# A layer's attention with its bookkeeping moved: another order of the modulation products, and the wide transposes copied out by two engines

## The reference

```
for i in range(DEPTH):                       # DEPTH = 2
    mods = sc @ ada_w[i] + ada_b[i]          # ada_w[i]: 1024 x 6144
    cmods = scc @ ada_w[i] + ada_b[i]
    x, xc = layer(x, xc, mods, cmods, ..., i < DEPTH - 1)

# in layer:
yb = conformer_conv(b_v, b_g, conv_b, conv_b_bias, cln_g, cln_b)
yc = window_attention(apply_rope(q_heads(c_q), cos, sin), apply_rope(kv_heads(c_k), cos, sin),
                      kv_heads(c_v), kc_c, vc_c, sink)
yd = global_attention(apply_rope(rms_norm(q_heads(d_q), qn_g), cos, sin),
                      apply_rope(rms_norm(kv_heads(d_k), kn_g), cos, sin),
                      kv_heads(d_v), kc_d, vc_d)
x_new = x + g1 * (jnp.concatenate([ya, yb, yc, yd], axis=-1) @ w_out)
```

## Time and profile before

| | us |
|---|---|
| median of three runs | 2913.59 |
| lowest and highest run | 2912.88, 2919.2 |
| the profiled execution | 2919.2 |
| its span in the trace | 2917.4 |
| attention of layer 0 (heads, flips, values) in the span | 221 to 397 |
| attention of layer 1 | 1315 to 1434 |

### The profile page before, as it was taken

The page is one execution under the profiler, slowest core; times in us unless marked ns, Lnnn a source line. Parts: engine busy times, 40 slices in busy tenths (PEclk is TensorE's granted clock), DMA queues, the critical chain, the costliest instruction groups (busy, mean ns, idle before and its releaser), DMA issues.

```text
span 2917.4 us, 35242 instructions
## 1 busy us (share of the span) xinstructions
PE 2636.4 (90%) x13904; PEld 1501.9 (51%) x13904; DVE 1283.0 (44%) x2508; ACT 979.0 (34%) x1825; POOL 334.1 (11%) x185
## 2 busy tenths in 40 slices
PE   5999897799999997796869999998699997999998
PEld 3875553323333322584534333332477686787886
DVE  2496514234444444476342232332656555343342
ACT  4216522233444443526422222221334333322222
POOL 0210001001111001120010000000013320121121
PEclk9999999799999999799989999999899998999999
DMA  6117723599999999320028999999221002232321
GB/s 244 58 58 261 256 77 130 198 322 350 348 360 361 345 347 317 106 73 1 15 94 331 386 387 386 387 386 386 89 87 44 12 16 76 80 102 87 96 85 51
DMA packets 303259, 568.50 MB, mean 195 GB/s; under 512 B 12656, under 2 KB 55792, under 8 KB 302968
## 3 DMA queue, kind: packets, MB, share of 16 engines
q1 hardware_dynamic: 294480, 545.33, 52.6%
q0 software_dynamic: 3840, 12.59, 1.8%
q10 hardware_dynamic: 4776, 8.33, 0.9%
HBM read 551.53 MB, written 14.68 MB: 194 GB/s over the span
## 4 chain that ended last, share of the span: by engine, by line
PE 41%; DMA 5%; DVE 4%; ACT 1%; issue 1%; POOL 0%; DVEq 0%; ACTq 0%; SPq 0%
PE PS L977 8%; PE PS L1080 4%; PE PS L1078 4%; PE PS L1079 4%; PE PS L1031 2%; PE PS L1091 2%; PE PS L1093 2%; PE PS L1092 2%; PE PS L926 2%; PE PS L1068 2%; DMA WIDE<-in_w_gate_dram 1%; DMA RING<-in_w_gate_dram 1%; PE PS L744 1%; PE PS L1195 1%; PE PS L1200 1%
## 5 line engine op out<-in xcount | busy, mean ns | idle before, releaser
L977 PE MATMUL PS<-RING,RF 128*64 128x512 f32 x1448 | 355.5, 617 | 12.5 <-DMA RING<-in_w_gate_dram 3.9
L977 PE MATMUL PS<-WIDE,RF 128*64 128x512 f32 x1408 | 332.2, 602 | 9.8 <-DMA WIDE<-in_w_gate_dram 3.8
L2535 POOL TENSOR_TENSOR WHL<-RING,WHL 128x1024 fp32r<-128x1024 f32 x57 | 153.9, 2700 | 1239.3 <-ACT WHL L1311 1239.3
L977 PEld LDWEIGHTS PS<-RING,RF 128*64 128x64 f32 x1448 | 93.2, 139 | 223.1 <-issue 203.4
L1078 PE MATMUL PS<-RR,WHL 128*128 128x512 f32 x512 | 204.5, 400 | 1.1 <-DVE RR L2288 1.1
L1080 PE MATMUL PS<-RR,WHL 128*128 128x512 f32 x512 | 203.6, 398 | 0.0
L1079 PE MATMUL PS<-RR,WHL 128*128 128x512 f32 x512 | 201.7, 394 | 0.0
L977 PEld LDWEIGHTS PS<-WIDE,RF 128*64 128x64 f32 x1408 | 92.8, 137 | 205.3 <-issue 182.5
L1542 ACT ACTIVATE RF<-PS,MODS,MSC 128x128 f32<-128x128 f32 x192 | 77.4, 438 | 305.0 <-PE PS L1031 158.5
L1311 ACT ACTIVATE WHL<-RING 128x1024 fp32r<-128x1024 f32 (+1 forms) x115 | 120.0, 1047 | 176.9 <-PE PS L1093 101.9
L1794 DVE TENSOR_TENSOR WHL<-RING,WHL 128x1024 fp32r<-128x1024 f32 (+1 forms) x58 | 71.6, 1234 | 197.5 <-ACT WHL L1311 197.5
(11 more groups left out here) (382 smaller groups left out, 4883.4 us busy)
## 6 DMA issues: line engine op xcount, KB each, us to landing
RING<-in_w_gate_dram SPq DMA_DIRECT2D x83, 1024.0 KB
WIDE<-in_w_down_dram SPq DMA_DIRECT2D x74, 1024.0 KB, 8.7
RING<-in_w_up_dram SPq DMA_DIRECT2D x70, 1024.0 KB
WIDE<-in_w_up_dram SPq DMA_DIRECT2D x57, 1024.0 KB, 11.6
RING<-in_w_down_dram SPq DMA_DIRECT2D x51, 1024.0 KB
RING<-in_ada_w_dram SPq DMA_DIRECT2D x48, 1024.0 KB
WIDE<-in_w_gate_dram SPq DMA_DIRECT2D x45, 1024.0 KB, 10.7
RING<-in_w_in_dram SPq DMA_DIRECT2D x30, 1024.0 KB
```

What stands on the lines that cost most here:

```text
L977: ins = e.matmul(a[r:r + 64, :], xs[:, j, 0:64], w[:, i, :], start=j < 2, stop=j > 5)
L2535: e.tensor_tensor(lo, load_buffer(loads[st["load"]])[:, js, cs], h.bitcast(F32), ALU.subtract).then_inc(pool, G(("lo", st["i"])))
```

## The change

In `attention_plan` the parts of a unit move. ada 0 and 1 stand behind the two middles of their round, ahead of the background pieces and of the second flip; ada 2 behind that flip and ahead of the values; ada 3 at the end of the round and ada 4 at the start of the next. The pieces that need bank 6 may now be taken at the first of the two places for background work in a round, between the middles and the second flip, and no longer at the second, behind the values.

In the engines' programs, a flip of more than four blocks is copied out by two engines: ScalarE takes columns 0 to 511, VectorE (new line 2067) the rest, 128 or 256 columns. TensorE waits for both before it uses either the banks or the copied rows. This holds for both layers: 8 items of mixer 0 and 16 of mixer 1 in each.

```diff
     def free_bank():
-        while need_ctx and not now[0]:
+        while need_ctx and now[0]:
             yield
...
         if 0 < n <= len(units):
-            plan.append(("ada", *units[n - 1], 2))
+            plan.append(("ada", *units[n - 1], 4))
...
-        if 0 < n <= len(units):
-            plan.append(("ada", *units[n - 1], 3))
         if n < pairs:
-            plan.append(("middle", i, *items[i]))
-        if 0 < n <= len(units):
-            plan.append(("ada", *units[n - 1], 4))
-        if n < pairs:
-            plan.append(("middle", i + 1, *items[i + 1]))
+            plan += [("middle", i, *items[i]), ("middle", i + 1, *items[i + 1])]
+        if n < len(units):
+            plan += [("ada", *units[n], 0), ("ada", *units[n], 1)]
         next(later, None)
         if 0 < n <= pairs:
             plan.append(("flip", i - 1, *items[i - 1]))
+        if n < len(units):
+            plan.append(("ada", *units[n], 2))
         if n > 1:
             plan.append(("values", i - 3, *items[i - 3]))
-        if n < len(units):
-            plan += [("ada", *units[n], 0), ("ada", *units[n], 1)]
         now[0] = 1
         next(later, None)
+        if n < len(units):
+            plan.append(("ada", *units[n], 3))
...
                         nb = b1 - b0 + 2
-                        o = bank(turns, ("eT", l, i), (A, ("eT", l, i)))
+                        also = [(V, ("eT", l, i))] if nb > 4 else []
+                        o = bank(turns, ("eT", l, i), (A, ("eT", l, i)), *also)
...
                         e.wait_ge(act, A["eT", l, i])
+                        if len(blocks) > 4:
+                            e.wait_ge(dve, V["eT", l, i])
...
-                        n1 = 128 * (b1 - b0 + 2)
+                        n1 = 128 * min(b1 - b0 + 2, 4)
...
+                    elif what == "flip":
+                        i, m, t, h = k
+                        b0, b1 = span(m, t)
+                        nb = b1 - b0 + 2
+                        if nb > 4:
+                            e.wait_ge(pe, P["eT", l, i])
+                            if i > 3:
+                                e.wait_ge(pe, P["pv", l, i - 4 + (i + 1) % 2])
+                            e.tensor_copy(ETB[i % 4][:, 512:nb * 128], held("eT", l, i)[:, 512:nb * 128]
+                                          ).then_inc(dve, V(("eT", l, i)))
```

More of the change, by code:

```diff
@@ L274, in attention_plan @@
         if 0 < n <= len(units):
-            plan.append(("ada", *units[n - 1], 2))
+            plan.append(("ada", *units[n - 1], 4))
         if i == nd:
-            now[0] = 1
             while not keys:
                 next(later)
-            now[0] = 0
         if n < pairs:
@@ L295, in attention_plan @@
             plan.append(("flip", i - 1, *items[i - 1]))
+        if n < len(units):
+            plan.append(("ada", *units[n], 2))
         if n > 1:
             plan.append(("values", i - 3, *items[i - 3]))
-        if n < len(units):
-            plan += [("ada", *units[n], 0), ("ada", *units[n], 1)]
         now[0] = 1
         next(later, None)
+        if n < len(units):
+            plan.append(("ada", *units[n], 3))
+    now[0] = 0
     for _ in later:
```

## The result

| | before | after |
|---|---|---|
| median of the timed runs, us | 2913.24 (2910.72 to 2919.20, 4 runs) | 2942.50 (2940.55 to 2946.46, 4 runs) |
| profiled execution: time, span, us | 2919.2, 2917.4 | 2940.74, 2938.9 |
| layer 0, first head to output projection | 175.9 | 197.4 |
| of it rounds 0-7, 8-11, 12-19, end | 57.5, 28.1, 70.5, 19.9 | 71.7, 27.4, 77.8, 20.5 |
| layer 1, first head to output projection | 118.3 | 124.7 |

The kernel became slower: ratio 1.0101, 95% interval 1.0085 to 1.0118. The forecast was 2931.5, with a range of 2906 to 2941; the direction was right and the time lies 1.5 us above the range. The two attention stretches grew by 21.5 + 6.4 = 27.9 us, nearly all of the 29.3 between the medians. (The two profiled spans differ by only 21.5: from the last head of layer 0 to the first of layer 1 the profile of before took 926.6 us, that of after 916.3.

A forecast was written before the change was run, and what follows sets the result against it. TensorE was taken as close to the bound in layer 0, a loop through one buffer in layer 1. 10.2 - 3.7 + 5.1 + 6.3 = +17.9, say +18: 2937 profiled, median forecast 2931.5, range 2906 to 2941.

The forecast's parts named there:

- Layer 1: Split flip copy: VectorE waits for the flip ahead of both maxima; mixer 1 +3.7, mixer 0 +2.6, in all +6.3 us.
- the right loop: Layer 0: head, flip, VectorE's copy, two middles, exponential, flip copy, row copy, transposes, head; 8.35 us against TensorE's 7.6.
- The keys, mean, var and spread products move ahead of the second flip, where bank 6 has been free for a while: Layer 0: these products stop waiting for VectorE's last multiply of the values; one such group held weight loads 6.0 us.
- Two of them go: Layer 0: bank 6 waits vanish and ada quarters cover the first flip's copy; 2.3 us of stalls go in rounds 8-11.
- the forecast's chain: Layer 0, rounds 17 to 19: ScalarE's gate copy (0.6) ahead of its flip copy; 8.9 against 8.69 us, +0.6.
- The forecast's sum for rounds 14 and 15: Layer 0: both scale steps fall between middle(29) and middle(30); 24.5 against 21.7 us, cost +2.8.
- rounds 0 to 2: Layer 0: round 0 holds a whole unit before head 1, +2.7 us; round 1 +0.4, round 2 +1.0.
- rival 3: Slower still: new gaps drop TensorE to its lower clock, three or four more starts of 2 us; +8, 2940; chance 0.13.
- transposes waiting for the row copy: Layer 0 sign: ada 3 ahead of the next head waits for ScalarE's row copy; row copy to transposes 0.73 us.
- the forecast's last part: Signs: layer 1 late rounds 6.3 us; layer 0 late rounds 8.9, keys and spread waits gone, rounds 8 to 11 in 24.4.
- Rival 1: Faster: layer 0 loses bank 6 stalls (-7), shorter flip copies gain in layer 1 (-2); 2905 us; chance 0.18.
- rival 2: Nearly even: ada chain has slack; layer 1 (+6) and scale rounds (+3) lost against -7 of stalls; +2, 2916; chance 0.14.

The follow-up runs named there:

- 6: Before's order, only the second flip of a round split between ScalarE and VectorE, against the kernel before: 2921.2 us, ratio 1.0025.
- 8: Before's plan with the first flip ahead of the head and all flips over four blocks split, against the kernel before: 2934.3 us, ratio 1.0068.
- 7: Before's plan without split, first flip of a round ahead of the head in both layers, against the kernel before: 2930.9 us, ratio 1.0062.
- 1: Before's order with the flip copy split between ScalarE and VectorE, against the kernel before: 2927.1 us, ratio 1.0045.
- 2: The new order without the split, ScalarE copying every flip whole, against the kernel before: 2932.9 us, ratio 1.0066.
- 11: The changed kernel with only second flips split; 2930.9 us, ratio 1.0057 to the kernel before.
- Experiment 5: The changed kernel with keys, mean, var and spread products back behind the values; 2955.7 us, ratio 1.0156 to the kernel before.
- 12: The changed kernel with rounds 0 to 2 of layer 0 in the old order; 2936.6 us, ratio 1.0076 to the kernel before.
- kernel 4: The changed kernel with row transposes (ada 3) back behind the next head and ada 4 behind the first middle; 2950.7 us, ratio 1.0124 to before.

## Why the prediction missed its range, step by step

The forecast was 11.0 us short. Of these 9.9 lie in layer 0, 0.1 in layer 1, and the rest outside the attention or in the scatter.

**Layer 1: right.** +6.4 against +6.3. Late rounds 6.43 (forecast 6.3), VectorE's copy 0.42 for 256 columns (0.43), mixer 0 rounds +0.42 (0.65). That the sum fits so closely is in part luck: rounds 3 to 6 gave 1.8 instead of 2.6 us, rounds 12 to 14 and the part behind the last head 2.9 instead of 2.05. The mechanism, VectorE's in-order wait ahead of the maxima, is shown from three sides: the split of second flips alone leaves the period at 5.75 (6), the same copy without a wait gains 0.21 us (8 against 7), and the split alone gives layer 1's loss entirely (1).

**Layer 0: the right loop, 9.9 us too small** (+21.5 against +11.6). By stretch:

| rounds | forecast | measured | difference |
|---|---|---|---|
| 0 to 2 | 23.3 | 26.4 | +3.1 |
| 3 to 7 | 44.5 | 45.3 | +0.8 |
| 8 to 11 | 24.4 | 27.4 | +3.0 |
| 12 to 16 | 48.9 | 49.2 | +0.3 |
| 17 to 19 | 26.7 | 28.6 | +1.9 |
| end | 19.9 | 20.5 | +0.6 |

**The step that failed** is "The keys, mean, var and spread products move ahead of the second flip, where bank 6 has been free for a while", and with it "Two of them go". The bank is free for the product, and the wait at the old place did go. But the next user of bank 6, the values, now comes right behind, and must wait until the product has been taken out of the bank: the keys and the gate by ScalarE, which has both exponentials in front, mean and var by VectorE's centring. The stall was moved from the product to the values, and there it lies on the way to the head. In rounds 8 to 11 TensorE's values wait 0.27 and 0.36 us for ScalarE's keys copy and 1.16 and 0.63 us for the centring, 2.4 of the 3.0 missed; the forecast had these rounds at TensorE's own work. This is read from the waits in the one profile, not from an experiment:
```profile
307.79 1.02 PE L862 MATMUL PS<-AR,CON 128*128 128x512 f32 x2
308.64 0.38 PE L889 MATMUL PS<-CON,RF 128*128 128x128 f32 x2
310.19 0.66 PE L902 MATMUL PS<-RF,AR 128*64 128x128 f32 x8 [1.16 <-DVE AR L2007]
```
The share of rounds 17 to 19 is shown by experiments 2 and 11: with the same order but the maxima in their old place the values do not wait, and these rounds take 8.66. In the changed kernel the forecast's chain ran from the gate copy over flip copy and row copy to the transposes, 8.95 from head to head; the longer one runs from the gate copy over the values (1.36 + 0.32) to the transposes, 9.53. Experiment 5 shows what the old place would win there: nothing, the head then waits for the spread. Whether another way round bank 6 would help was not tried. (The forecast's sum for rounds 14 and 15 writes 16.2 where its terms add up to 16.3, which changes nothing.)

**The term that was mis-sized** is rounds 0 to 2. The gap behind the first quarters was forecast (round 0 7.2, measured 7.81); its price on the clock stood in rival 3 and not in the sum. TensorE there, after:
```profile
220.59 1.92 PE L757 MATMUL PS<-RING,S 128*32 128x512 f32 x16
225.56 1.84 PE L749 MATMUL PS<-SM,TM 128*128 128x2 f32 x8 [3.05 <-ACT TM L1320]
227.33 1.23 PE L879 MATMUL PS<-RF 64*128 64x256 f32 x4
...
230.38 2.89 PE L757 MATMUL PS<-RING,S 128*32 128x512 f32 x16
```
After 3.05 us idle the transposes took 1.84 instead of 1.05 and the next quarters 2.89 instead of 1.92. The granted clock, 0.94 before, was 0.75 here (1.2 for much of the stretch instead of 2.4 GHz), and 0.94 again once these rounds had the old order (12). Kernels 2, 5 and 11 run the same program in these three rounds, with the same gap of 3.05 us, and took 24.4, 26.3 and 26.1 us at a granted clock of 0.87, 0.75 and 0.81. So at most some 1 us of the 3.1 is a longer chain and some 2 the clock, and how much the clock takes differs from one execution to the next.

**Right as forecast:** transposes waiting for the row copy (11.9 us, the longest entry of TensorE's waits for another engine), rounds 14 and 15 in 24.2 us (24.5), TensorE idle 1.65 and 2.85 us on either side of a flip before round 15's quarters (about 5), round 16 8.40 (8.5). Round 12 took 8.27 instead of 7.5, which the others of its stretch made up. The waits of keys and spread on the multiply went, as the forecast's last part said, and still the rounds were not shorter: that sign alone did not test the step. Rival 1, the free gain of shorter copies, failed on the wait and not on the copy; rival 2 failed on the loop; rival 3, by its cause, came true for the first rounds, and by its figure of 2940 it is the nearest to the measured time, though only some 2 us of the miss are traced to the clock.

What stays open: the rest of the difference between the medians (29.3 against 27.9), which is within the scatter of the long stretch between the attentions, and the last 0.6 us of rounds 8 to 11.

## What to carry to other kernels

When a product is moved to where its buffer is free, look up the next user of that buffer and the engine that empties it: a stall moved behind a busy in-order engine comes back on whoever is next. Before an engine gets a share of another's copy, look at what stands behind it in its own queue, for the wait costs more than the copy. And of two steps that share a bank (quarters and transposes), moving one alone makes it wait for the other (24.2 us in kernel 4); where a copy holds TensorE, try first to put independent TensorE work in the gap (here it took the late rounds of layer 1 from 5.75 to 5.08 us, though the total did not show it).

## What the runs showed of the hardware

ScalarE and VectorE read neighbouring banks of one PSUM pair at the same moment without slowing each other: 0.60 us for 512 columns beside VectorE, 0.59 alone; VectorE's copy out of PSUM took 0.42 for 256 and 0.28 for 128 columns.

The clock after a gap is not the same each time. In layer 1, where kernels 6 and 11 are the same program, both have a gap of 5.71 us ahead of the head of round 11, and TensorE then runs at the lower level for a while, though not for the same while; of kernel 6, then of kernel 11:
```profile
1391.96 2.08 PE L882 MATMUL PS<-RF 64*128 64x512 f32 x4 [5.71 <-ACT RF L1439]
...
1397.30 1.54 PE L892 MATMUL PS<-CON,RF 128*128 128x128 f32 x6 [0.90 <-ACT RF L1452]
```
```profile
1398.87 2.08 PE L879 MATMUL PS<-RF 64*128 64x512 f32 x4 [5.71 <-ACT RF L1436]
...
1404.21 0.88 PE L889 MATMUL PS<-CON,RF 128*128 128x128 f32 x6 [0.90 <-ACT RF L1449]
```
The second flip takes 1.54 us in the one and 0.88 in the other after the same 5.71 us of waiting. That one round came out 2.0 us apart, as much as many of the effects studied here. Rounds 0 to 2 of layer 0 show the same in the four kernels with one program there: after one and the same gap of 3.05 us they took between 24.4 and 26.4 us.
